# A hybrid Hyena/GLA/S5 block on one core: where four products of the gate weights stand beside S5's loop and Hyena's convolutions

## The reference

```python
h = rmsnorm(x, g_norm1) * (1 + sc1) + sh1
k_l, v_l, a_l, u_l, q_l, r_l, hy_l, gate_l = split_cols(h @ w_in, COL_SIZES)
y_gla = gla_readout(...)     # gated linear attention, both directions
y_s5  = s5_readout(...)      # S5 state space layer, both directions, then GELU and a GLU product
y_hy  = hyena_mix(hy_l, ...) # x2 * conv(x1 * conv(v)): two long convolutions by FFT
m = sigmoid(g_hy) * (y_hy @ w_hy) + sigmoid(g_gla) * (y_gla @ w_gla) + sigmoid(g_s5) * (y_s5 @ w_s5)
x = x + gt1 * (m @ w_out)
x = x + gt2 * swiglu(rmsnorm(x, g_norm2) * (1 + sc2) + sh2)
```

## Time and profile before

| | |
|---|---|
| median of 3 runs | 1235.68 us (1232.58 to 1236.21) |
| the profiled execution | 1235.91 us, its span 1234.1 us |
| TensorE (PE) busy | 1118.5 us, 91% of the span, mean granted clock 0.944 |
| weight loads (PEld) | 849.1 us, 69% |
| VectorE (DVE) busy | 585.3 us, 47% |
| ScalarE (ACT) busy | 401.7 us, 33% |
| GpSimd (POOL) busy | 336.3 us, 27% |

### The profile page before, as it was taken

One profiled execution on the slowest core, in us unless ns is written; L12 is line 12 of the kernel. 1 busy time (PEld: TensorE's weight loads), 2 busy tenths in 40 slices (PEclk: granted clock), 3 DMA queues, 4 the chain that ended last, 5 costly groups with the idle time before them and its releaser, 6 DMA issues.

```text
span 1234.1 us, 15748 instructions
## 1 busy us (share of the span) xinstructions
PE 1118.5 (91%) x6109; PEld 849.1 (69%) x6109; DVE 585.3 (47%) x1134; ACT 401.7 (33%) x763; POOL 336.3 (27%) x293
## 2 busy tenths in 40 slices
PE   4789989978989999898997979997999999999995
PEld 1358958866657676677473754696888888888884
DVE  3684156576488878882296957235000011000013
ACT  2572323543344534432521100234232212332221
POOL 3022312502200000000221210342555655655540
PEclk9889999988889999998997989797999999999998
DMA  9802223765132323314333236652333233333211
GB/s 332 274 28 76 69 69 127 129 151 170 37 92 77 95 52 86 86 56 119 125 95 109 69 136 209 207 148 69 96 85 93 94 94 103 103 103 103 67 53 69
DMA packets 139512, 134.32 MB, mean 109 GB/s; under 512 B 13082, under 2 KB 126010, under 8 KB 138413
## 3 DMA queue, kind: packets, MB, share of 16 engines
q1 hardware_dynamic: 126432, 105.51, 29.3%
q0 software_dynamic: 3904, 16.15, 3.6%
q10 hardware_dynamic: 9100, 11.64, 3.1%
HBM read 120.18 MB, written 11.01 MB: 106 GB/s over the span
## 4 chain that ended last, share of the span: by engine, by line
PE 57%; DVE 13%; issue 3%; ACT 2%; DMA 1%; ACTq 1%; POOL 0%; DVEq 0%; POOLq 0%
PE psum L731 50%; PE psum L991 1%; PE psum L1094 1%; PE psum L971 1%; DVE ring_lo L2038 1%; DMA buf<-in_w_out 1%; PE psum L984 1%; PE psum L764 1%; DVE buf L2114 1%; ACTq L1566 1%; DVE hT_lo L2375 1%; PE psum L959 1%; DVE buf L2084 1%; DVE buf L2289 1%; DVE buf L2087 0%
## 5 line engine op out<-in xcount | busy, mean ns | idle before, releaser
L1282 POOL TENSOR_TENSOR ring_lo<-buf,ring_hi 128x512 fp32r<-128x512 f32 (+2 forms) x220 | 280.7, 1308 | 514.0 <-ACT ring_hi L1437 514.0
L731 PE MATMUL psum<-hT_hi,ring_hi 128*128 128x512 f32 x712 | 285.3, 401 | 7.7 <-DVE hT_lo L2375 3.5
L731 PE MATMUL psum<-hT_lo,ring_hi 128*128 128x512 f32 x712 | 279.1, 392 | 0.0
L731 PE MATMUL psum<-hT_hi,ring_lo 128*128 128x512 f32 x712 | 278.9, 392 | 0.0
L1437 ACT ACTIVATE ring_hi<-buf 128x512 fp32r<-128x512 f32 (+1 forms) x260 | 139.6, 610 | 229.4 <-PE psum L731 161.2
L731 PE MATMUL psum<-buf,buf 128*128 128x512 f32 (+1 forms) x368 | 153.9, 577 | 21.5 <-issue 15.5
L731 PEld LDWEIGHTS psum<-hT_hi,ring_hi 128*128 128x128 f32 x712 | 135.0, 190 | 42.2 <-issue 5.1
L731 PEld LDWEIGHTS psum<-hT_lo,ring_hi 128*128 128x128 f32 x712 | 134.9, 190 | 28.5 <-issue 1.7
L731 PEld LDWEIGHTS psum<-hT_hi,ring_lo 128*128 128x128 f32 x712 | 134.8, 189 | 28.6
L731 PEld LDWEIGHTS psum<-buf,buf 128*128 128x128 f32 x368 | 69.9, 209 | 96.4 <-issue 87.3
L2384 DVE TENSOR_TENSOR buf<-psum,buf 128x512 f32<-128x512 f32 x22 | 15.2, 692 | 221.1 <-PE psum L731 221.1
(11 more groups left out here) (335 smaller groups left out, 1717.4 us busy)
## 6 DMA issues: line engine op xcount, KB each, us to landing
buf<-in_w_in SPq DMA_DIRECT2D x26, 1024.0 KB, 5.4
buf<-in_w_mod SPq DMA_DIRECT2D x24, 1024.0 KB, 6.8
buf<-in_w_ffn_in SPq DMA_DIRECT2D x44, 512.0 KB, 5.2
buf<-in_w_ffn_out SPq DMA_DIRECT2D x8, 1024.0 KB, 5.1
scr_k<-buf POOLq DMA_DIRECT2D x4, 1024.0 KB, 5.2
buf<-scr_k POOLq DMA_DIRECT2D x4, 1024.0 KB, 8.0
buf<-in_w_out SPq DMA_DIRECT2D x4, 1024.0 KB, 5.4
buf<-in_w_ffn_out SPq DMA_DIRECT2D x4, 768.0 KB, 4.5
```

The source lines that it names most:

```text
L731: ins = nc.tensor.matmul(o, a, b, start=start and n == 0, stop=stop and n == len(pairs) - 1)
L1282: nc.gpsimd.tensor_tensor(ring_lo[:, a:a + n], ring[:, a:a + n], ring_hi[:, h + i * n:h + i * n + n].bitcast(fp32), SUB)\
```

## The change

The order of the products changes in four places, and nothing else.

- In the loop, Hyena's first four gate products (gate00 and gate01, two halves each) are taken out of the list beside it, and gate00's two halves stand at its end. 24 products are left of 26.
- Product B is placed only where m % 3 is 0 (six turns) instead of where it is not 2 (eleven turns).
- What is left after the loop (gate00's two halves) is placed ahead of `s5_y` of the last block; before, `s5_y` came first, and only an evacuation was left.
- Gate01's two halves join the list beside the convolutions, whose order changes, and a second `one_beside` stands between `uunfold` and `yinv` of each convolution.

```diff
         early, ms = ms[:6], ms[6:]
-        beside = ms[:2] + hy[:2] + kept[:2] + ms[2:6] + hy[2:4] + kept[2:4] + hy[4:6] + ms[6:10] + hy[6:8] \
-            + hy[8:10] + hy[10:12]
+        beside = ms[:2] + hy[:2] + ms[2:6] + hy[2:4] + hy[4:6] + ms[6:10] + hy[6:8] \
+            + hy[8:10] + hy[10:12] + kept[:2]
...
-            one_beside(m % 3 != 2)
+            one_beside(m % 3 == 0)
             if m + 2 < 2 * NB:
                 step("s5_w", *divmod(m + 2, 2))
                 step("s5_k", *divmod(m + 2, 2))
-        step("s5_y", NB - 1)
         while late or beside:
             one_beside()
+        step("s5_y", NB - 1)
...
-        beside = [ms[1], ms[3]] + kept[4:6] + ms[4:8] + kept[6:8] + ms[8:]
+        beside = [ms[1], ms[3]] + kept[2:4] + ms[4:8] + kept[4:6] + ms[8:12] + kept[6:8] + ms[12:]
...
             step("uunfold", cv)
+            one_beside()
             one_beside()
             step("yinv", cv)
```

## The result

The changed kernel takes 1252.13 us (median of its runs, 1251.02 to 1254.68) against 1235.65 (1232.58 to 1236.21) for the kernel before: ratio 1.0142, 95% interval 1.0126 to 1.0159. It is slower, by twice the 8.3 us that were forecast; the range ended at 1251. The profiled execution took 1251.1 us with a span of 1249.3, 15.2 longer than the profiled one of before. A line Ln of the kernel before is L(n+1) here.

The account below looks back on a forecast made before the run. TensorE was taken to bound the kernel, but not everywhere: waits with VectorE set the loop's turns. GLU 10.1 us later and Hyena's -1.8 made +8.3 on 1235.91: 1244.2 us, 0.7% slower; 8 in 10 for 1235 to 1251.

Parts of the forecast that it names:

- twelve turns: S5's loop, from one `s5_v`'s end to the next: 172.5 us become 166.1, saving 6.4 of 22.8 us.
- wait for gate00's `low`: Loop's end: TensorE waits for ScalarE 0.75, VectorE's evacuation 1.55, `low` 2.4, plus 1.0 for GpSimd's split (bounds 0 to 4.9).
- two gates, with the clock: Loop's end: gate00's two products take 11.4 us plus 1.7 for the lower clock after the idle (bounds 0 and 3).
- `s5_y` 7's end to GLU: Behind the loop: evacuation, store, load and GELU until the GLU product take 18.4 us, before and after alike.
- part 2: The loop's end: new wait and two gates ahead of `s5_y` 7 make GLU start 10.1 us later.
- `s5_y` and hy_tok at full clock: Between loop and GLU: running these at full clock brings nothing, since ScalarE's and the DMA's way is longer.
- the chain: Turns with `s5_y`: `s5_k`, product A (first `one_beside`), `s5_d`, `s5_y`, `s5_v` take 13.3 us at full clock; 14.2 taken.
- TensorE's wait for L2087: Sign in the loop: TensorE's wait for `s5_v` grows from 8.8 us to over 20.
- bound by TensorE's sum: Rival: the loop's turns shrink with the work, all 22.8 us leave, 1224 us; chance 0.13.
- Hyena's part: Beside the convolutions: two products hidden in TensorE's gaps, splits cost +1.0, clock gains 0.9 and 1.9; net -1.8 us.
- more locks: Rival: gate00's `low` stands through GpSimd's whole split (+3.9), both Hyena splits hit VectorE (+3.4); 1251 us, chance 0.10.
- The clock holds: Rival: TensorE resumes at full clock after idling, in loop, gates and inverses; +0 to +3, 1237.5 us, chance 0.14.

Follow-up runs that it names:

- e7: The kernel before, with GpSimd's two loads of hy_tok held back until the load of scr_y has landed; 1235.1 us, ratio 1.0002.
- e8: The changed kernel with product B back in two turns of three and GpSimd's two hy_tok loads held back until scr_y's load has landed; 1229.51 us, ratio 0.9967.
- e10: The kernel before with gate01's pair moved beside Hyena's convolutions and GpSimd's two hy_tok loads held back until scr_y's load has landed; 1226.57 us, ratio 0.9934.
- e3: The changed kernel with GpSimd's two loads of hy_tok held back until the load of scr_y has landed; 1245.57 us, ratio 1.0088.
- e2: The changed kernel with gate00's low part on GpSimd and not VectorE; 1242.46 us, ratio 1.0068.
- e11: The changed kernel with gate00's low part on GpSimd and GpSimd's two hy_tok loads held back until scr_y's load has landed; 1238.65 us, ratio 1.0033.
- e12: The changed kernel with `s5_y` 7 ahead of gate00's products, gate00's low part on GpSimd, and GpSimd's hy_tok loads held back behind scr_y's; 1233.63 us, ratio 0.9993.
- e1: The changed kernel with `s5_y` 7 put back ahead of gate00's two products at the loop's end; 1246.63 us, ratio 1.0097.
- e6: The changed kernel without the added product ahead of each inverse transform, the two products falling behind the second inverse; 1266.86 us in one execution.
- e4: The changed kernel with the loop's product B back in two turns of three, the pair beside Hyena's convolutions staying moved; 1238.65 us, ratio 1.0041.
- e5: The kernel before with only gate01's pair moved from the loop to the places beside Hyena's convolutions; 1237.8 us, ratio 1.0026.
- e9: The changed kernel with `s5_y` 7 ahead of gate00's two products and gate00's low part on GpSimd; 1244.05 us, ratio 1.0076.

## Why the prediction was wrong, point by point

The direction and its mechanism were right: the loop does not shrink with its work, and two gates put ahead of `s5_y` 7 push GLU back. The size was wrong. By its terms GLU was to start at 600.8, and it started at 610.8. Term by term, forecast and measured:

| term | forecast | measured |
|---|---|---|
| up to the first turn's start | 0 | +1.46, in the part where both kernels are the same |
| twelve turns | 166.1 | 168.1 |
| last `s5_v` to hy 5 1's end | 23.2 | 23.7 |
| wait for gate00's `low` | 5.7 | 7.21 |
| two gates, with the clock | 13.1 | 12.9 |
| `s5_y` 7 | 3.3 | 3.1 |
| `s5_y` 7's end to GLU | 18.4 | 23.3 |
| GLU to the second inverse's end, against before | -1.8 | -1.4 |
| from there to the span's end, against before | 0 | -3.5 |

**The step that failed** is in part 2: that from the end of `s5_y` 7 to GLU "the way is ScalarE's and the DMA's", 18.4 us and the same after as before. It measured 23.3, half of the 10 us by which GLU came later than forecast. It was taken as one way with a fixed length, and it is the longer of two. In the kernel before both were about 18.4: e7, e8 and e10, whose loads landed in 5.2 to 6.6 us, still take 18.2 to 18.4, and there it is TensorE's way alone. In the changed kernel ScalarE's load, 0.06 us ahead of GpSimd's first before, stood 0.24 behind, the landing went from 7.3 to 12.3 us, and that way became 23.3. With GpSimd held back (e3) it falls to 20.0, which is TensorE's way with the two gates at the lower clock; e3 takes 6.6 us less, of which the traces give this 3.3. That `s5_y` and hy_tok at full clock bring "nothing" was wrong in the same place: hy_tok is done sooner, TensorE's wait behind it is longer, and the two gates run slower, some 1.5 us in all, which the load hides. The prediction looked at what each queue is moved past, but at no transfer that is issued beside the load.

The other half of the 10 us is spread over the start, the turns and the wait for `low`. The end gave 3.5 back, so the 15.2 us between the spans are closer to the forecast than the terms are, by luck.

**The wait for `low`** was the term most in doubt. I took +1.0 for GpSimd's split beside it; the two operations took 4.53 us for 2.4, so +2.1, inside my bounds of 0 and 4.9. By the Trainium skill ("SBUF — State Buffer", section "SBUF: two separate sides"), where each half waits for one GpSimd operation at most, I had worked out some 2 us; the trace gives 2.1, and my choice against the rule was wrong. GpSimd paid too: its split took 6.90 us, and 5.04 in e2, where no `low` stood beside it. The rest of the 7.2 us was ScalarE's 0.7, VectorE's 1.6, as written, and some 0.4 between them. e2 shows the whole wait with its clock to be worth 9.5 us, the largest item.

**The turns.** A still stands in each and the chain was right; 168.1 lies in the bounds. Of the four turns taken at 14.2 us three took 15.0 to 15.1 and one 13.3: the row of 14.86, which I had gone below, was the better guess. Such a turn takes 13.3 or about 15, and which it is can change between traces with the same loop: e2 has three of 13.3 or 13.4 where the changed kernel has one. The forecast also said that TensorE's wait for L2087 would be over 20 us: it is 15.9, because part of the idle time fell on `s5_w` (12.4, before 5.6 by the same view), which I had not named. The rival "bound by TensorE's sum" is out: its turns would have been under 13.3.

**Hyena's part** was right in kind. Where GLU ran at full clock it is 140.8 and 141.3 us from GLU to the second inverse's end without the pair (before, e7), and 137.7 to 139.8 with it (e10, e8, e11, after, e3, e12, e1). The two further splits of GpSimd, feared with up to 4.4 us, show no loss in that sum.

**The end** came out 3.5 us better than before, which no term had. The work there is the same, and the difference is clock: from 45 to 61 us behind the inverse the granted clock was 0.76 before (777.7 to 793.7) and 0.87 after (796.4 to 812.4), from 100 to 140 us behind it 0.83 and 0.91. The stretch takes from 499.0 to 502.6 us in the traces of all kernels but e6, and in the first of these windows e1 and e4 have 0.76 as well. But before and e7, the two without the pair, are at the top of that, so whether the pair has a part in it stays open.

**The rival "more locks"** named 1251, near the result, by luck: of its 3.9 us at `low` 1.1 came, of its 3.4 at Hyena nothing. "The clock holds" is out: the granted clock in the loop was 0.89 and had been 0.97.

So the change is three things: the pair at Hyena, a gain; B's absence, which shortens the loop by 4.4 us and leaves gate00's two products in the open behind it; and the loop's end, where mending its three waits (e12) takes back 18.5 us. The second is a loss even with all waits mended: e12 takes 4.1 us more than e8, in which B stands in the loop. The best kernel, e10, keeps the first alone and orders the loads.

**Open** stays what sets the two issues 0.06 us one way round in the kernel before and 0.21 to 0.24 the other in after, e2, e4, e5 and e6; both wait for the stores of scr_y. One trace of the kernel before shows its order. That the order decides is read from the table and not tested by itself: e3's wait holds GpSimd back until the load has landed, and no run puts the load just ahead. What speaks for it is e5 against before: but for the stores of scr_y, which the load waits for, and GpSimd's four loads, no transfer is issued from 15 us ahead of the load to 11 behind it in either. And e11's executions scatter from 1233.9 to 1242.8 us, without a cause that its one profile shows; that profile is of its quickest execution, whose first `s5_v` ended at 341.7, 2.5 us sooner than before's.

## What to carry to other kernels

When work moves across a chain that ends in a load, write down what else is issued in the same microsecond on the other queues: a landing time taken from a trace may hold for that order alone. Where two ways end together, as at GLU in the kernel before, price both. Work of TensorE that fills its idle stretch in a loop bound by another engine gives back little when it goes (4.4 us of 22.8); count what leaves the other engine. Put such work where TensorE stands anyway, as beside these convolutions, where two products were worth some 13 us (e6, one execution). A mend that failed or gave half (e1, e5, e9) had in each case uncovered the next wait in the same chain: try it with that next wait mended before discarding it.

## What the runs showed of the hardware

The load of 1 MB from ScalarE's queue landed in 5.2 to 7.3 us when nothing of GpSimd's was issued ahead of it or when that was 15.6 us ago (e1), and in 12.2 to 14.4 us when GpSimd's 3 MB were issued 0.2 to 4.4 us ahead. By the Trainium skill ("DMA: Bandwidth & Descriptors", section "Queues, rings and completion order") each DMA engine takes turns between the queues that have work, a packet at a time. That fits with the load being slowed by the others; that 0.06 us ahead or 0.24 behind should decide between 7.3 and 12.3 us, the rule does not tell.

GLU's products took 13.9 to 14.0 us at a granted clock of 1.00, and 15.7 to 16.6 where TensorE had stood before them (e5: 0.84). After an idle stretch of 3.43 us before GLU (after) the clock stayed up, after 3.59 (e2) and 3.58 (e6) it did not; but after the 3.04 us before the two gates (after) it fell to 0.87 as well. So the length of the stretch alone does not tell here, and of a short stretch before a long run of products both outcomes have to be priced.
